# Transposes moved inside a projection half, a value product moved behind a branch unit, and one wait on Pool moved down

## The chip, the cores and the metric

The kernel runs on one core of a Trainium2 chip. The metric is the device time of one execution in microseconds (us): the median of three runs. Engines are named as in the profile: PE is TensorE (PEld its weight loads), ACT is ScalarE, DVE is VectorE, POOL is GpSimd, SP is the engine that issues most DMAs.

## The reference

Two layers of a decoder trunk on 256 tokens of width 1024 (float32), then a final norm. Each layer adds a mixer block and a mixture of experts:

```
h = rmsnorm(x);  proj = h @ w_in                      # 1024 x 7076
y_a = dsa_attention(...)        # 64 keys per query picked by an indexer, softmax
y_b = chunked_sgu(...)          # u * (tril(W_s) norm(v) + b)
y_c = stick_breaking_attention(...)
y_d = short_gated_conv(...)
merged = sum over n of sigmoid(gate_logits[n]) * (y_n @ w_branch[n])
x = x + merged @ w_out
x = x + hierarchical_moe(rmsnorm(x))   # top 1 of 4 groups, top 2 of its 8 experts
```

Stick-breaking attention forms, for head and query t, weights `A[t,s] = beta[t,s] * prod over s<j<t of (1 - beta[t,j])`, and multiplies them with the values. The gated branch is y_b.

## The kernel before

Tokens are held as two row tiles of 128 (`t` = 0, 1). The mixer's weights come as 36 units of 1 MB (`MIXER_UNITS`), each used in two halves `v` (unit u has halves 2u and 2u+1). A unit is either a slice of `w_in` (512 columns by four 128-row chunks), one branch's `w_branch`, or a quarter of `w_out`. Units come into a ring of nine slots. For each half, ACT rounds the weights to a high part (`hi_half`, line 1146), DVE forms the remainder (`lo_half`, line 1673, count `lo_done`), and PE multiplies in three passes (`three`, lines 492 to 494). Four halves of split weights are kept.

PE runs through a list written out by hand. `in_half(v, use)` waits until `lo_half(v)` is done, and then for each row tile issues six matmuls of 512 columns (two chunks, three passes); `use` picks PSUM banks 0 and 1, or 2 and 3. The first half of a block also waits that the block two uses back has been read out (`emptied`, count `block_out`). `wide_unit` multiplies a branch's output with its `w_branch`: twelve matmuls a half, into banks 0 and 1 and then 2 and 3; it has an `emptied` wait before each pair of banks.

Between these stand the small products of the attentions. Around the change the list is, in each layer:

```
                    in_half(32, 9)
                    pe.wait_ge(*L(zexp, 2))
                    p_transposes(zc, 1, 4)
                    pe.wait_ge(*L(yb_done, 1))
                    y_transposes(y_ab, 6)
                    in_half(33, 9)
```

Then come `pv(vc, 1, 7)` (16 small matmuls of weights by values into bank 7), `wide_unit(17)` (the branch product of y_b), `y_transposes(y_c, 5)`, `logits(qkT_a, 0, 6)`, units 18 and 19, units 20 and 21 (with `p_transposes(sc, 0, 6)` between them), and so on. `p_transposes(zc, 1, 4)` (line 602) turns the second row tile's stick-breaking weights, which ACT's exponential (`stick_exp(1)`, line 1188) has written; `y_transposes(y_ab, 6)` (line 487) turns y_b, which DVE's `sgu_gate` has written.

Every engine works through its own queue in its written order. DVE's queue around the change: `stick_sums(1)`, `y_evac_c(0)`, `sgu_gate`, `lo_half(33)`, `lo_half(34)`, `gate(0, 8)`, `yT_low(2, 1, 6)`, `lo_half(35)`, two rounds of `top_rounds` (the indexer's selection), `y_evac_c(1)` (line 1811: copies what `pv(vc, 1, 7)` made, count `y_out`), `gate(1, 9)` (line 1849), one more round, `lo(18)` (halves 36 and 37), `yT_low(3, 0, 5)` (line 1696, waits for ACT's `yT_high(2, 0, 5)`), two rounds, `lo(19)`, `sparse_logits(0, 6, sc)`, three rounds, `select_mask(1)`, `lo(20)`, `sparse_logits(1, 4, zc)`, `gate(2, 12)`, `lo(21)`, `lo(22)`.

ACT's queue: `stick_exp(1)`, `token_evac(8)` (line 1152: reads block 8 out of banks 0 and 1 through a sigmoid), `p_evac(2, 1, 4)`, `yT_high(1, 1, 6)` (line 1167), `hi_half(35)`, `token_evac(9)` (banks 2 and 3, after `gate(0, 8)`), `hi(18)`, `block_evac(10)` (after `gate(1, 9)`), `yT_high(2, 0, 5)`, `block_evac(11)`, `hi(19)`.

POOL adds the gated branches into `merged` (line 1560, count `gate_sum`); the fifth such sum is awaited by PE ahead of half 62, the first half of unit 31, which does not read `merged`; `m_transposes(0)` behind that half does.

Expert weights are loaded by SP's queue (lines 382 and 396) behind the mixer's units, each as its place comes free. They fill seven places for gate and up weights and nine for down weights before the first expert is computed.

Of the kernel before, what the change touches and what calls it, by code (L numbers as in the profile page):

```python
# [10 lines left out]
ACT = mybir.ActivationFunctionType  # L11
# [100 lines left out]
def build(nc, x_in, positions, norm1_g, w_in, sgu_ln_g, sgu_ln_b, w_spatial, b_spatial, conv_w, w_branch,  # L112
          w_out, norm2_g, w_rg, b_rg, w_re, b_re, w_eg, w_eu, w_ed, norm_f_g, out):
    ctx = ExitStack()
    with ctx:
# [306 lines left out]
        def preload_sqrt():  # L422

            nc.scalar.activation(spare, eps_t[:], ACT.Sqrt)

        def preload_gelu():

            nc.scalar.activation(spare, eps_t[:], ACT.Gelu_apprx_tanh)
# [40 lines left out]
        with nc.Block() as whole:  # L469

            @whole.tensor
            def _(pe):
# [7 lines left out]
                for l in range(DEPTH):  # L480
# [29 lines left out]
                    def in_half(v, use, layout="natural", between=None):  # L510

                        b0 = 2 * (use % 2)
                        h = MIXER_UNITS[v // 2][3]
                        n = unit_cols(v // 2)
                        pe.wait_ge(*L(lo_done, v + 1))
                        chunks = [(4 * h + 2 * (v % 2) + k, k) for k in range(2)]
                        begin, end = chunks[0][0] == 0, chunks[-1][0] == C - 1
                        if begin and use >= 2:
                            emptied(use - 2)
                        outs = []  # L520
                        if layout == "natural":
                            for t in range(TT):
                                outs.append((ps[:, b0 + t, 0:n], lambda c, k, t=t: h_tile(c, t),
                                             lambda c, k: w_tile(v, k, 0, n), True))
                        elif layout == "transposed":
                            for m in range(4):
                                outs.append((ps[:, b0 + m // 2, T * (m % 2):T * (m % 2) + T],
                                             lambda c, k, m=m: w_tile(v, k, P * m, P),
                                             lambda c, k: h_tile(c), m % 2 == 0))
                        else:  # L530
                            for t in range(TT):
                                outs.append((ps[:, b0, BW * t:BW * t + BW], lambda c, k, t=t: h_tile(c, t),
                                             lambda c, k: w_tile(v, k, 0, BW), t == 0))
                            for m in range(2):
                                outs.append((ps[:, b0 + 1, T * m:T * m + T],
                                             lambda c, k, m=m: w_tile(v, k, BW + P * m, P),
                                             lambda c, k: h_tile(c), m == 0))
                        if v < 4:
                            for c, k in chunks:
                                pe.wait_ge(*L(xT_lo, XT_GROUP_OF[c] + 1))  # L540
                                for dst, st, mv, opens in outs:
                                    ins = three(dst, st(c, k), mv(c, k), begin and k == 0 and opens,
                                                end and k == 1)
                                if k == 0 and between is not None:
                                    between()
                        else:
                            for dst, st, mv, opens in outs:
                                for c, k in chunks:
                                    ins = three(dst, st(c, k), mv(c, k), begin and k == 0 and opens,
                                                end and k == 1)  # L550
                        ins.then_inc(half_used, 1)

                    def in_unit(u, use, layout="natural"):
                        in_half(2 * u, use, layout)
                        in_half(2 * u + 1, use, layout)

                    def wide_unit(u, use, st, first_, last_):

                        for v in (2 * u, 2 * u + 1):
                            pe.wait_ge(*L(lo_done, v + 1))  # L560
                            final_half = v == 2 * NU - 1
                            order = [(hf, t) for hf in range(2) for t in range(TT)]
                            if final_half:
                                order.sort(key=lambda o: o[1])
                            for n, (hf, t) in enumerate(order):
                                if first_ and v % 2 == 0 and t == 0:
                                    emptied(use + hf - 2)
                                ins = three(ps[:, 2 * hf + t, :], st(v % 2, t), w_tile(v, 0, 512 * hf, 512),
                                            first_ and v % 2 == 0, last_ and v % 2 == 1)
                                if final_half and n == 1:  # L570
                                    ins.then_inc(mid_mm, 1)
                                elif first_ and last_ and v % 2 == 1 and n == 1:
                                    ins.then_inc(wide_mm, 1)
                            ins.then_inc(half_used, 1)
# [24 lines left out]
                    def p_transposes(src, t, b0):  # L599
                        for b in range(t + 1):  # L600
                            for h in range(NH):
                                ins = nc.tensor.transpose(ps[:, b0 + b, P * h:P * h + P],
                                                          src[:, h, P * b:P * b + P], ident[:])
                        ins.then_inc(pT_mm, 1)
# [10 lines left out]
                    def y_transposes(y, b0):  # L615
                        transposes([ps[:, b0, T * k + P * t:T * k + P * t + P]
                                    for k in range(2) for t in range(TT)],
                                   [y[:, t, P * k:P * k + P] for k in range(2) for t in range(TT)], yT_mm)

                    def y_tile(ring_at):  # L620
                        return lambda k, t: (yT_hi[:, ring_at, k, P * t:P * t + P],
                                             yT_lo[:, ring_at, k, P * t:P * t + P])
# [81 lines left out]
                    for g in range(NG):  # L704
                        ins = mm(ps[:, 6, P * g:P * g + P], wsT[:, g, :], vn[:, :, HD * g:HD * g + HD],
                                 start=(g == 0), stop=True, skip_group_check=True)
                    ins.then_inc(sgu_mm, 1)
                    in_half(32, 9)
                    pe.wait_ge(*L(zexp, 2))
                    p_transposes(zc, 1, 4)  # L710
                    pe.wait_ge(*L(yb_done, 1))
                    y_transposes(y_ab, 6)
                    in_half(33, 9)
                    pe.wait_ge(*L(pT_out, 2))
                    pe.wait_ge(*L(y_out, 1))
                    pv(vc, 1, 7)
                    pe.wait_ge(*L(yT_lo_out, 2))
                    wide_unit(17, 10, y_tile(1), True, True)
                    pe.wait_ge(*L(y_out, 2))
                    y_transposes(y_c, 5)  # L720
                    logits(qkT_a, 0, 6, la_mm)
                    in_unit(18, 12)
                    pe.wait_ge(*L(yT_lo_out, 3))
                    logits(qkT_a, 1, 4, la_mm)
                    in_unit(19, 12)
# [20 lines left out]
                    in_unit(28, 20)  # L746
                    in_unit(29, 20)
                    in_unit(30, 21)
                    pe.wait_ge(*L(gate_sum, 5))

                    def m_transposes(c0):
                        for b in range(2):
                            transposes([ps[:, 4 + c0 // 2 + b, T * k + P * t:T * k + P * t + P]
                                        for k in range(2) for t in range(TT)],
                                       [merged[:, t, P * (c0 + 2 * b + k):P * (c0 + 2 * b + k) + P]
                                        for k in range(2) for t in range(TT)], xT_mm)

                    in_half(62, 21)
                    m_transposes(0)
                    in_half(63, 21)  # L760
                    pe.wait_ge(*L(xT_lo, 7))
# [345 lines left out]
            def _(act):  # L1107
# [12 lines left out]
                for l in range(DEPTH):  # L1120
# [64 lines left out]
                    def stick_exp(t):  # L1185
                        w = P * (t + 1)
                        act.wait_ge(*L(zarg, t + 1))
                        A(zc[:, :, 0:w], zc[:, :, 0:w], ACT.Exp).then_inc(zexp, 1)
# [82 lines left out]
                    hi(16)  # L1271
                    hi_half(34, l)
                    stick_exp(1)
                    token_evac(8, sig, 0, ACT.Sigmoid)
                    p_evac(2, 1, 4)
                    yT_high(1, 1, 6)
                    hi_half(35, l)
                    act.wait_ge(*L(gate_prod, 1))
                    token_evac(9, sig, 2, ACT.Sigmoid)
# [330 lines left out]
            def _(dve):  # L1610
# [51 lines left out]
                for l in range(DEPTH):  # L1662
# [259 lines left out]
                    sgu_gate()  # L1922
                    lo_half(33)
                    lo_half(34)
                    gate(0, 8)
                    yT_low(2, 1, 6)
                    lo_half(35)
                    top_rounds(1, 2)
                    y_evac_c(1)
# [273 lines left out]
```

## Time and profile before

| | us |
|---|---|
| median of three runs (lowest, highest) | 889.68 (889.56, 890.39) |
| profiled execution, device time | 889.39 |
| its span, first to last instruction | 887.6 |
| PE busy in the span | 826.1 (93%) |
| DVE busy | 529.8 (60%) |
| ACT busy | 386.5 (44%) |
| POOL busy | 117.3 (13%) |

The mixer of the first layer takes the span from about 25 to 235 us, its experts up to about 443; the second layer follows with the same order. Times in the rows below are microseconds from the span's start. PE's 0.39 us for a matmul of 512 columns is its latency; one starts every 0.23 us.

### The profile page before, as it was taken

How to read it: one execution, taken by the hardware profiler on the slowest of the kernel's cores; microseconds unless marked ns; L12 is line 12 of the kernel's file. 1: busy time of each engine (PE TensorE's matmuls, PEld its weight loads, DVE VectorE, ACT ScalarE, POOL GpSimd, SP SyncE). 2: the span in 40 equal slices, each digit the busy share in tenths (PEclk: the TensorE clock that was granted, in tenths of full speed). 3: DMA queues.
4: the chain of work that ended last, by engine and by line, in shares of the span. 5: the costliest groups of instructions: out<-in, count | busy, mean ns of one | idle time of the engine just before them, and what ended most of it. 6: DMA issues, size and time to landing. Idle time of an engine off the chain costs nothing.

```text
span 887.6 us, 20367 instructions
## 1 busy us (share of the span) xinstructions
PE 826.1 (93%) x8763; PEld 662.0 (75%) x8763; DVE 529.8 (60%) x1067; ACT 386.5 (44%) x669; POOL 117.3 (13%) x169
## 2 busy tenths in 40 slices
PE   7999999999999998877999999999999999977984
PEld 7898878887897775655589977788789876654652
DVE  5768698667555555423376778976566455534434
ACT  5546868545422222111275568774454222211113
POOL 2840101212000000000066001022200000000000
PEclk9999999999999999978999999999999999999888
DMA  9966545498969999999998463555987999999994
GB/s 305 389 222 160 174 144 188 143 381 322 396 267 418 419 418 420 419 421 420 402 374 294 151 207 123 173 174 222 408 313 282 415 420 420 417 421 419 421 419 183
DMA packets 64125, 281.47 MB, mean 317 GB/s; under 512 B 5120, under 2 KB 7248, under 8 KB 39712
## 3 DMA queue, kind: packets, MB, share of 16 engines
q1 hardware_dynamic: 62752, 278.45, 80.1%
q0 software_dynamic: 800, 1.40, 1.2%
q8 instruction: 71, 1.16, 0.5%
q10 hardware_dynamic: 480, 0.28, 0.1%
q14 instruction: 22, 0.18, 0.1%
HBM read 279.06 MB, written 1.05 MB: 316 GB/s over the span
## 4 chain that ended last, share of the span: by engine, by line
PE 61%; DMA 20%; SPq 6%; issue 5%; ACT 3%; DVE 3%; POOL 1%; DVEq 0%; ACTq 0%; POOLq 0%
PE ps L492 12%; PE ps L494 11%; PE ps L493 11%; DMA ring<-in_w_exp_up 10%; PE ps L825 8%; DMA late<-in_w_exp_down 6%; PE ps L812 5%; PE ps L841 4%; SPq L382 4%; DMA late<-in_w_exp_up 3%; PE ps L925 2%; SPq L396 2%; DMA ring<-in_w_in 2%; POOL wide L1560 1%; PE ps L831 1%
## 5 line engine op out<-in xcount | busy, mean ns | idle before, releaser
L1673 DVE TENSOR_TENSOR split_lo<-ring,split_hi 128x1024 fp32r<-128x1024 f32 (+1 forms) x142 | 196.1, 1417 | 42.0 <-ACT split_hi L1146 40.8
L492 PE MATMUL ps<-split_hi,hT_hi 128*128 128x512 f32 (+2 forms) x416 | 161.4, 388 | 3.1 <-DVE hT_lo L1683 1.4
L1146 ACT ACTIVATE split_hi<-ring 128x1024 fp32r<-128x1024 f32 (+1 forms) x144 | 145.5, 1049 | 29.5 <-PE ps L494 27.3
L493 PE MATMUL ps<-split_lo,hT_hi 128*128 128x512 f32 (+2 forms) x416 | 157.6, 379 | 0.0
L494 PE MATMUL ps<-split_hi,hT_lo 128*128 128x512 f32 (+2 forms) x384 | 145.2, 378 | 0.0
L2085 DVE TENSOR_TENSOR wsT<-mb,ps 32x64 f32<-32x64 f32 x256 | 54.9, 215 | 141.2 <-ACT mb L1356 138.5
L1356 ACT ACTIVATE mb<-ps 128x64 f32<-128x64 f32 x64 | 14.3, 223 | 243.7 <-PE ps L825 243.7
L492 PEld LDWEIGHTS ps<-split_hi,hT_hi 128*128 128x128 f32 x416 | 78.2, 188 | 21.8 <-issue 3.7
L493 PEld LDWEIGHTS ps<-split_lo,hT_hi 128*128 128x128 f32 x416 | 78.3, 188 | 12.9
L494 PEld LDWEIGHTS ps<-split_hi,hT_lo 128*128 128x128 f32 x384 | 72.2, 188 | 13.3
L1577 POOL TENSOR_TENSOR idx<-idx,wt 128x128 f32<-128x128 f32 x32 | 12.1, 399 | 393.8 <-PE ps L847 309.8
L1383 ACT ACTIVATE first_down<-ps 32x256 f32<-32x256 f32 x112 | 41.8, 373 | 48.6 <-PE ps L841 48.0
L812 PEld LDWEIGHTS ps<-idx,wide 128*128 128x128 f32 x512 | 58.4, 192 | 5.8 <-issue 5.7
L812 PE MATMUL ps<-idx,wide 128*128 128x128 f32 x512 | 61.2, 278 | 0.0
L825 PE MATMUL ps<-ring,qkr 128*32 128x128 f32 x1536 | 51.7, 291 | 9.9 <-DMA ring<-in_w_exp_up 9.9
L825 PEld LDWEIGHTS ps<-ring,qkr 128*32 128x32 f32 x1536 | 44.9, 117 | 17.6 <-DMA ring<-in_w_exp_up 11.1
L2119 DVE COPY first_down<-ps 32x256 f32<-32x256 f32 x112 | 47.5, 424 | 14.6 <-PE ps L841 13.8
L825 PE MATMUL ps<-ring,yy 128*32 128x128 f32 x1344 | 45.1, 291 | 11.6 <-DMA ring<-in_w_exp_up 11.6
L1560 POOL TENSOR_TENSOR wide<-wide,qkr 128x1024 f32<-128x1024 f32 x10 | 33.1, 3310 | 165.2 <-DVE qkr L1849 165.2
L925 PE MATMUL ps<-first_down,wr 128*128 128x512 f32 x112 | 54.4, 618 | 0.0
L825 PEld LDWEIGHTS ps<-ring,yy 128*32 128x32 f32 x1344 | 39.2, 118 | 20.1 <-DMA ring<-in_w_exp_up 15.0
L2098 DVE TENSOR_TENSOR x<-x,ps 128x512 f32<-128x512 f32 x56 | 38.5, 688 | 15.7 <-PE ps L925 15.7
(278 smaller groups left out, 1317.9 us busy)
## 6 DMA issues: line engine op xcount, KB each, us to landing
ring<-in_w_in SPq DMA_DIRECT2D x52, 1024.0 KB, 10.0
ring<-in_w_exp_gate SPq DMA_DIRECT2D x45, 1024.0 KB, 24.5
ring<-in_w_exp_up SPq DMA_DIRECT2D x45, 1024.0 KB, 26.1
late<-in_w_exp_down SPq DMA_DIRECT2D x38, 1024.0 KB, 26.4
ring<-in_w_exp_down SPq DMA_DIRECT2D x15, 1024.0 KB, 26.7
new_pair<-in_w_exp_gate SPq DMA_DIRECT2D x10, 1024.0 KB, 18.6
new_pair<-in_w_exp_up SPq DMA_DIRECT2D x10, 1024.0 KB, 20.9
late<-in_w_exp_gate SPq DMA_DIRECT2D x9, 1024.0 KB, 24.6
```

The costliest lines, as they stand in the source:

```text
L492: mm(dst, st[0], mv[0], start=start, stop=False, skip_group_check=True)
L493: mm(dst, st[0], mv[1], start=False, stop=False, skip_group_check=True)
L494: return mm(dst, st[1], mv[0], start=False, stop=stop, skip_group_check=True)
L812: ins = mm(ps[:, b, P * c:P * c + P], wide[:, t, P * cc:P * cc + P], pick[:, t, :], start=(t == 0), stop=(t == TT - 1), skip_group_check=True)
L825: ins = mm(ps[32 * j:32 * j + 32, b, 0:P], hg[:, c, SLOTS * i:SLOTS * i + SLOTS], w[:, :, c, 64 * j:64 * j + 64], start=(c == 0), stop=(c ...
L925: mm(bank(banks[k]), scatT[:, t, :], y_slots[g % 2][:, 512 * hf:512 * hf + 512], start=True, stop=True).then_inc(scat_mm, 1)
L1146: A(half_view(split_hi[:, v % SPLITS, :], v), raw_half(v, l), ACT.Copy).then_inc(hi_done, 1)
L1383: ins = A(y_slots[g % 2][SLOTS * i:SLOTS * i + SLOTS, 256 * q:256 * q + 256], ps[32 * q:32 * q + 32, down_bank(e), 0:256], ACT.Copy)
L1560: nc.gpsimd.tensor_tensor(m, m, sig[:], ALU.add).then_inc(gate_sum, 1)
L1673: V.tensor_tensor(half_view(split_lo[:, v % SPLITS, :], v), raw_half(v, l), half_view(split_hi[:, v % SPLITS, :], v).bitcast(F32), ALU.sub ...
L2085: ins = V.tensor_tensor(hid[:, par, 64 * j:64 * j + 64], silu[32 * j:32 * j + 32, par, :], ps[32 * j:32 * j + 32, b, 64:128], ALU.mult)
L2119: ins = V.tensor_copy(y_slots[g % 2][SLOTS * i:SLOTS * i + SLOTS, 256 * q:256 * q + 256], ps[32 * q:32 * q + 32, down_bank(e), 0:256])
```

## The change

- PE: the transposes of y_b and of the second row tile's stick-breaking weights are put inside `in_half(33)`, between its two row tiles, with y_b's first; the function `in_half` gets a place for this.
- PE: `pv(vc, 1, 7)` is put behind `wide_unit(17)`. `y_transposes(y_c, 5)` and the first `logits(qkT_a, ...)` come behind the first half of unit 18 instead of ahead of it.
- PE: the wait for POOL's fifth sum is put behind `in_half(62)`.
- ACT: a small sigmoid on one column behind `stick_exp(1)`; `yT_high(1, 1, 6)` goes ahead of `token_evac(8)` and `p_evac(2, 1, 4)`.
- DVE: `yT_low(2, 1, 6)` goes ahead of `gate(0, 8)`. Nothing else of DVE's queue is changed.

```diff
+        def preload_sigmoid():
+
+            nc.scalar.activation(spare, eps_t[:], ACT.Sigmoid)
...
                         else:
-                            for dst, st, mv, opens in outs:
+                            for nth, (dst, st, mv, opens) in enumerate(outs):
+                                if nth == 1 and between is not None:
+                                    between()
                                 for c, k in chunks:
...
+                    def second_tile():
+                        pe.wait_ge(*L(yb_done, 1))
+                        y_transposes(y_ab, 6)
+                        pe.wait_ge(*L(zexp, 2))
+                        p_transposes(zc, 1, 4)
+
                     in_half(32, 9)
-                    pe.wait_ge(*L(zexp, 2))
-                    p_transposes(zc, 1, 4)
-                    pe.wait_ge(*L(yb_done, 1))
-                    y_transposes(y_ab, 6)
-                    in_half(33, 9)
+                    in_half(33, 9, "natural", second_tile)
+                    pe.wait_ge(*L(yT_lo_out, 2))
+                    wide_unit(17, 10, y_tile(1), True, True)
                     pe.wait_ge(*L(pT_out, 2))
                     pe.wait_ge(*L(y_out, 1))
                     pv(vc, 1, 7)
-                    pe.wait_ge(*L(yT_lo_out, 2))
-                    wide_unit(17, 10, y_tile(1), True, True)
+                    in_half(36, 12)
                     pe.wait_ge(*L(y_out, 2))
                     y_transposes(y_c, 5)
                     logits(qkT_a, 0, 6, la_mm)
-                    in_unit(18, 12)
+                    in_half(37, 12)
...
-                    pe.wait_ge(*L(gate_sum, 5))
...
                     in_half(62, 21)
+                    pe.wait_ge(*L(gate_sum, 5))
                     m_transposes(0)
...
                     stick_exp(1)
+                    preload_sigmoid()
+                    yT_high(1, 1, 6)
                     token_evac(8, sig, 0, ACT.Sigmoid)
                     p_evac(2, 1, 4)
-                    yT_high(1, 1, 6)
                     hi_half(35, l)
...
+                    yT_low(2, 1, 6)
                     gate(0, 8)
-                    yT_low(2, 1, 6)
```

## Rows read from the trace of the kernel before

**Rows 1.** Windows: stretch, its length, busy of PE, PEld, DVE, ACT, POOL, PEclk, DMA, GB/s.

```profile
128.00:160.00 32.00, 32.00 (x154) 25.78 (x153) 27.71 (x37) 25.20 (x40) 6.63 (x2) 1.00 0.48 164
```

**Rows 2.** Timeline of PE about unit 16: start, us, line, count, [idle before <- releaser].

```profile
114.10 1.09 PE L602 MATMUL ps<-ident,ring 128*128 128x128 f32 x8 [1.39 <-ACT ring L1188]
115.03 0.60 PE L487 MATMUL ps<-ident,yy 128*128 128x128 f32 x4
115.51 0.50 PE L492 MATMUL ps<-split_hi,hT_hi 128*128 128x512 f32 x1
...
118.37 1.89 PE L610 MATMUL ps<-first_down,ring 128*128 128x64 f32 x16
120.07 0.48 PE L492 MATMUL ps<-split_hi,yT_hi 128*128 128x512 f32 x1
...
548.24 1.09 PE L602 MATMUL ps<-ident,ring 128*128 128x128 f32 x8 [1.40 <-ACT ring L1188]
```

**Rows 3.** Timeline of DVE, unit 16's second half to unit 18's first.

```profile
114.25 2.35 DVE L1673 TENSOR_TENSOR split_lo<-ring,split_hi 128x1024 fp32r<-128x1024 f32 x2
...
122.11 0.42 DVE L1811 COPY yy<-ps 128x256 f32<-128x256 f32 x1
...
124.56 2.36 DVE L1673 TENSOR_TENSOR split_lo<-ring,split_hi 128x1024 fp32r<-128x1024 f32 x2
```

**Rows 4.** Timeline of ACT: the sigmoids of blocks 8 and 9.

```profile
115.36 1.27 ACT L1152 ACTIVATE qkr<-ps,scal 128x512 f32<-128x512 f32 x2
...
118.84 1.28 ACT L1152 ACTIVATE qkr<-ps,scal 128x512 f32<-128x512 f32 x2
```

**Rows 5.** Timeline of PE: y_c's transposes, then first matmuls of halves 36, 42 and 43.

```profile
125.65 0.60 PE L487 MATMUL ps<-ident,yy 128*128 128x128 f32 x4
...
126.82 0.50 PE L492 MATMUL ps<-split_hi,hT_hi 128*128 128x512 f32 x1
...
144.92 0.47 PE L492 MATMUL ps<-split_hi,hT_hi 128*128 128x512 f32 x1
...
147.86 0.50 PE L492 MATMUL ps<-split_hi,hT_hi 128*128 128x512 f32 x1
```

**Rows 6.** Timeline of DVE: `yT_low(3)`, `lo(20)`, `lo_half(43)`, then `y_evac_a(0)`.

```profile
126.91 0.69 DVE L1696 TENSOR_TENSOR yT_lo<-ps,yT_hi 128x512 fp32r<-128x512 f32 x1
...
137.02 2.36 DVE L1673 TENSOR_TENSOR split_lo<-ring,split_hi 128x1024 fp32r<-128x1024 f32 x2
...
144.37 3.44 DVE L1673 TENSOR_TENSOR split_lo<-ring,split_hi 128x1024 fp32r<-128x1024 f32 x1
...
151.75 0.49 DVE L1837 TENSOR_TENSOR yy<-ps,scal 128x128 f32<-128x128 f32 x2 [1.68 <-PE ps L610]
```

**Rows 7.** Timeline of POOL: the first and the fifth sum.

```profile
143.39 3.33 POOL L1560 TENSOR_TENSOR wide<-wide,qkr 128x1024 f32<-128x1024 f32 x1 [37.31 <-DVE qkr L1849]
...
201.94 3.29 POOL L1560 TENSOR_TENSOR wide<-wide,qkr 128x1024 f32<-128x1024 f32 x1 [13.55 <-DVE qkr L1849]
```

**Rows 8.** Timeline of PE ahead of half 62, and of DVE's `lo_half(63)`.

```profile
204.28 0.39 PE L494 MATMUL ps<-split_hi,hT_lo 128*128 128x512 f32 x1
205.28 0.50 PE L492 MATMUL ps<-split_hi,hT_hi 128*128 128x512 f32 x1 [0.60 <-POOL wide L1560]
...
202.91 3.40 DVE L1673 TENSOR_TENSOR split_lo<-ring,split_hi 128x1024 fp32r<-128x1024 f32 x1
```

**Rows 9.** Windows at the start of the first layer's experts (columns as in Rows 1).

```profile
248.00:250.00 2.00, 2.00 (x20) 2.00 (x19) 1.19 (x5) 0.00 (x0) 0.75 (x2) 1.00 0.00 0
```

**Rows 10.** Timeline of PE among the experts: 64 equal matmuls after waits of different length.

```profile
349.76 1.95 PE L825 MATMUL ps<-ring,yy 128*32 128x128 f32 x64 [1.30 <-DMA ring<-in_w_exp_up]
357.25 3.37 PE L825 MATMUL ps<-ring,yy 128*32 128x128 f32 x64 [3.94 <-DMA ring<-in_w_exp_up]
...
844.33 3.15 PE L825 MATMUL ps<-new_pair,yy 128*32 128x128 f32 x64 [2.07 <-DMA new_pair<-in_w_exp_up]
```

**Rows 11.** Windows after the wait that ended at 357.25 (columns as in Rows 1).

```profile
358.00:360.00 2.00, 2.00 (x44) 1.85 (x40) 0.00 (x0) 0.00 (x0) 0.00 (x0) 0.50 1.03 430
```

## Prediction

> **What bounds the kernel.** I read the windows by stage first, to see which engine is full where: in the mixer about the change PE is busy for the whole of a 32 us stretch at the full clock [rows 1]. The chain of waits there is PE after PE, so what is added to PE's queue or holds it lengthens the layer, unless the experts behind take it back. The waits of PE in the mixer name two that the change is aimed at: 1.39 us before the transposes of the stick-breaking weights, released by ACT's exponential [rows 2], and 0.60 us before half 62, released by POOL [rows 8]. Then I read the timelines of PE, DVE and ACT side by side about both, because PE's waits alone show only who came last, and not who would be next. Both layers do the same: the transposes start at 114.10 and at 548.24 with the same wait [rows 2], so what I work out for the first layer counts twice. POOL and SP issue nothing that is moved; no DMA is.
>
> **Step 1: the wait for the exponential goes, and DVE's remainder takes its place.** Half 33 needs `lo_half(33)`. DVE works two of these from 114.25 in 2.35 us, so the first is done about 115.45 [rows 3]. Half 33 started at 115.51 [rows 2], a few hundredths later. So the transposes stood in a gap in which PE could not have started half 33 anyway, and they are what filled it. After the change PE is free at 114.10 − 1.39 = 112.71 and still waits for 115.5: an idle of 2.8 us. Nothing on DVE ahead of that point depends on what is moved. Gain: 0.
>
> **Step 2: the transposes now cost their time.** They took from 114.10 to 115.51, 1.41 us. Inside half 33 they stand between matmuls for which all is ready. Both of their inputs are written by then. Half 33 ends at 118.37 + 1.41 = 119.8. Loss: 1.4.
>
> **Step 3: block 9's read-out is late for unit 17.** y_b's transposes now start after half of half 33 (its 12 matmuls took 118.37 − 115.51 = 2.86), at 116.94, and the last ends 0.60 later, at 117.5 [rows 2]. ACT waits for them with everything behind `yT_high(1)`: the sigmoid of block 8, `p_evac(2)`, `hi_half(35)`, the sigmoid of block 9. The same four items took 118.84 − 115.36 = 3.48 from the start of the first to the start of block 9's [rows 4], in another order. So block 9's sigmoid starts at about 117.6 + 3.5 = 121.1 and ends at 122.4. Unit 17 can start at 119.8 and wants banks 2 and 3 six matmuls later, at 121.2. Loss: 1.2. The small sigmoid itself costs nothing: it and its table load lie in ACT's idle between the exponential's end at 114.1 and 117.5; without that cover it would be the 1.3 us load, which is in ACT's queue before too. Unit 17 takes 125.65 − 120.07 = 5.58 [rows 2, 5] and ends at 119.8 + 1.2 + 5.6 = 126.6. `yT_low(2)`, earlier on DVE, is ready at about 118.9 and holds nothing.
>
> **Step 4: the value product now stands just ahead of half 36, with DVE's queue between them.** On DVE `y_evac_c(1)` is ahead of `gate(1, 9)`, one selection round and `lo_half(36)`. Before, the copy started at 122.11 and `lo(18)` at 124.56, 2.45 later, the first half done 1.2 after that [rows 3]; PE was at unit 17 meanwhile. Now the product starts at 126.6, PE is free of it 1.70 later at 128.3, and its result is there 1.89 after its start, at 128.5 [rows 2]. Half 36 can start at 128.5 + 2.45 + 1.2 = 132.2. PE idles 3.9 us. `block_evac(10)`, which half 36 also needs, waits for the same `gate(1, 9)`; it would be done at about 131.3, so it is the next in line and not the last. y_c's transposes and the first logits (126.82 − 125.65 = 1.17 [rows 5]) are only exchanged with half 36. PE is now 1.4 + 1.2 + 3.9 = 6.5 late.
>
> **Step 5: DVE is later than PE, and PE meets it again.** `yT_low(3)` started 126.91 − 125.65 = 1.26 after y_c's transposes [rows 5, 6]. These now come after half 36, at 132.2 + 2.8 = 135.0, so `yT_low(3)` starts at 136.3, 9.4 later than before. DVE idles from 133.4 till then, since its queue is in order. From `yT_low(3)` to `lo_half(43)` DVE had no gap before: it did `lo_half(43)` until 144.37 + 3.44 = 147.81, and PE started half 43 at 147.86 [rows 5, 6]. With no slack there, PE's lag of 6.5 must grow to DVE's 9.4: I expect 1.9 before half 40 (there the slack was 0.9: `lo_half(40)` done at 137.02 + 1.2 = 138.2, and the half started two halves of 2.7 and four transposes of 0.4 before 144.92, at 139.1), and 0.4 each before halves 42 and 43. After that DVE idled 1.68 before `y_evac_a(0)` [rows 6], so PE leads again and the lag stays at 9.4. Loss in steps 2 to 5 together: 9.4 a layer.
>
> `lo_half(43)` counts with 3.44, as in its row, and not with 1.22: it ran beside POOL's sum, which began at 143.39 for 3.33 us [rows 6, 7], and this sum moves with `gate(2, 12)`. The Trainium skill, SBUF — State Buffer, in its part on engine ports, calls the port pair of VectorE and GpSimd an exclusive lock, where the loser blocks fully. By that rule the remainder would run only when POOL is done, at 146.72, and end at 147.9, which the trace bears out at 147.81; had the two shared it instead, or not met, the sum would be up to 0.4 a layer less.
>
> **Step 6: the wait for POOL.** Unit 30 is issued to 204.28 + 0.23 = 204.51, half 62 started at 205.28. `lo_half(62)` was done when `lo_half(63)` began, at 202.9, so half 62 can follow at once. POOL's sum was done at 205.23 [rows 7], before the half's end at 207.3; `lo_half(63)` at 202.91 + 3.40 = 206.31 [rows 8], in time too. Nobody else's order changes. Gain: 0.8 a layer. If that cover were gone, the gain would be 0 and nothing lost.
>
> **Step 7: TensorE's clock.** The idles of 2.8 and 3.9 us are new to the mixer; the longest there was 1.39, with the clock at 2.4 GHz on both sides. Among the experts 64 matmuls took 1.95 after an idle of 1.30, but 3.15 after one of 2.07 and 3.37 after one of 3.94 [rows 10], at a granted clock of 0.50, the level of 1.2 GHz [rows 11]. All ten idles over 2 us there were followed by such a slow group. A fall costs 1.2 to 1.4 by these rows. Bounds for the two new idles: 0 (stay at full clock, as after 1.39) and 1.7 each; I take 1.3 each, since 3.9 is at the row of 3.94 and 2.8 lies between the rows of 2.07 and 3.94. What PE loses there, the transposes behind it, ACT and DVE lose too, so it adds to the 9.4. For the 1.9 before half 40 I take nothing.
>
> The Trainium skill, TensorE: Matmul & The Clock Gate, on HAM oscillation, says that a TensorE left waiting falls back to half rate and pays again for each such wait, a rule that speaks against this change; the same page warns that where the switch falls varies from run to run. By the rule the sum has the 2.6, without it not. The trace agrees in the 3.15 and 3.37 against 1.95.
>
> **Do the experts take the lag back?** Their stretch is limited by loads in part. But when the first is computed, the DMA share is 0.00 [rows 9]: all places are full, and the next load waits for the first expert. So the loads are late by what PE is late, and the lag stays whole.
>
> **The sum.** A layer: 1.4 + 1.2 + 3.9 + 2.9 = 9.4, less 0.8, plus 2.6, is 11.2. Two layers: 22.4. Against the profiled execution's 889.4 that gives 911.8; it lies 0.3 under the median of the runs, so I say 912.
>
> **Rivals.**
> - The clock stays up, or falls once a layer: 889.4 + 2 × 8.6 = 906.6, or 909.2. For it: before these idles PE was denser than among the experts. Against: ten of ten.
> - More queues meet: the first softmax or the sigmoids of blocks 12 and 13 become late too, or the clock falls a third time (1.9 before half 40). Another 2 to 3 a layer: 916 to 918. Against: `p_transposes(sc, 0, 6)` stands two units behind its logits.
> - The other side: the experts absorb it. Place: the first loads of the experts, issued behind the mixer. If DMA were behind when the experts start, a mixer later by 11 us would let the loads gain as much against PE. It decides once DMA has 11 us of loads pending at that start; then the time is 889.4 or under, 888. Against it: the share of 0.00.
> - The change does what it is aimed at: `lo_half(33)` is ready early, the 1.4 and the 0.8 go, and the product finds DVE ahead: 889.4 − 2 × 2.2 = 885. Against: 115.45 beside 115.51, and the order of DVE's queue.
>
> **How the numbers follow.** Forecast 50%, clock better 30%, more queues 14%, absorbed 3%, works as aimed 3%. The range reaches from 904 (no fall of the clock, 906.6, and step 3 at nothing, 2 × 1.2 less) to 917. Runs of this kernel can be told apart from about 0.2%, 1.8 us. Faster 0.04 (the last rival, and most of the absorbed case), same 0.02, slower 0.94.
>
> **What would show it.** After the change PE's waits should have: about 2.8 before half 33, released by DVE's split_lo; about 1.2 inside unit 17, released by ACT's sigmoid (qkr); about 3.9 before half 36, released by split_lo; about 2 before half 40, both layers; none on POOL's sum. DVE should idle about 4 before `y_evac_c(1)` and about 3 before `yT_low(3)`. The granted clock should show 0.50 behind half 33's and half 36's start. The forecast is wrong if half 36 starts within 1 us of the product's end, or if the experts' loads start earlier against the first expert than before.

## The result, and the profile after

The changed kernel takes 913.38 us (median of five runs, 912.68 to 915.11) against 889.66 for the kernel before, a ratio of 1.027 (95% interval 1.0256 to 1.0284): 24 us slower. Forecast were 912, slower, in a range of 904 to 917. The profiled execution took 913.89 with a span of 912.2, 24.6 more than before.

What PE waited for in the first layer's mixer, in the changed kernel (engine, line and tile, what released it: us in total, times, longest):

```profile
PE ps L496 <- DVE split_lo L1684: 8.8, 5, 3.8
PE ps L496 <- ACT qkr L1162: 1.2, 1, 1.2
PE ps L496 <- issue: 0.2, 1, 0.2
```

The wait for the exponential [rows 2] is gone, and so is the one for POOL [rows 8]. In their place stand four waits for DVE's remainders and one for ACT's read-out of block 9. (The fifth wait for a remainder in the count, of 0.17 us, is the one ahead of the kernel's very first unit, at 24.13, which was 0.48 in the kernel before.) The timeline of PE shows where (start, us, line, shape, count, [idle before <- releaser]); lines 496 to 498 are the 492 to 494 of before, 491 the 487, 608 the 602, 616 the 610:

```profile
115.12 0.80 PE L496 MATMUL ps<-split_hi,hT_hi 128*128 128x512 f32 x1 [2.81 <-DVE split_lo L1684]
117.85 0.81 PE L491 MATMUL ps<-ident,yy 128*128 128x128 f32 x4
118.49 1.04 PE L608 MATMUL ps<-ident,ring 128*128 128x128 f32 x8
119.29 0.47 PE L496 MATMUL ps<-split_hi,hT_hi 128*128 128x512 f32 x1
120.75 0.40 PE L496 MATMUL ps<-split_hi,yT_hi 128*128 128x512 f32 x1
123.52 0.50 PE L496 MATMUL ps<-split_hi,yT_hi 128*128 128x512 f32 x1 [1.21 <-ACT qkr L1162]
127.74 1.89 PE L616 MATMUL ps<-first_down,ring 128*128 128x64 f32 x16
133.46 0.79 PE L496 MATMUL ps<-split_hi,hT_hi 128*128 128x512 f32 x1 [3.83 <-DVE split_lo L1684]
138.74 0.61 PE L491 MATMUL ps<-ident,yy 128*128 128x128 f32 x4
151.39 0.50 PE L496 MATMUL ps<-split_hi,hT_hi 128*128 128x512 f32 x1 [1.72 <-DVE split_lo L1684]
160.94 0.50 PE L496 MATMUL ps<-split_hi,hT_hi 128*128 128x512 f32 x1 [0.29 <-DVE split_lo L1684]
```

Five of the forecast's waits are to be read off: before half 33 (2.81), in unit 17 (1.21), before half 36 (3.83), before half 40 (1.72) and before half 43 (0.29). The 0.4 forecast before half 42 shows only as a larger distance: the half starts 0.62 after the four transposes ahead of it (156.97 to 157.59) and not 0.35. The second layer has the same five waits: 2.81, 1.00, 3.83, 1.73 and 0.33. DVE's own timeline has the two idles that answer to [rows 3] and [rows 6]:

```profile
113.86 2.35 DVE L1684 TENSOR_TENSOR split_lo<-ring,split_hi 128x1024 fp32r<-128x1024 f32 x2
119.33 0.69 DVE L1707 TENSOR_TENSOR yT_lo<-ps,yT_hi 128x512 fp32r<-128x512 f32 x1 [3.12 <-ACT yT_hi L1177]
129.73 0.42 DVE L1822 COPY yy<-ps 128x256 f32<-128x256 f32 x1 [4.32 <-PE ps L616]
130.08 1.21 DVE L1860 TENSOR_TENSOR wide<-qkr,br 128x1024 f32<-128x1024 f32 x1
132.18 2.36 DVE L1684 TENSOR_TENSOR split_lo<-ring,split_hi 128x1024 fp32r<-128x1024 f32 x2
140.02 0.69 DVE L1707 TENSOR_TENSOR yT_lo<-ps,yT_hi 128x512 fp32r<-128x512 f32 x1 [5.47 <-ACT yT_hi L1177]
```

DVE does nothing for 4.32 us while PE works on unit 17, then copies the product, and only then makes the remainder that PE has been waiting for. Its second idle, before `yT_low(3)`, is 5.47 where about 3 was forecast: the forecast had half 36 at full clock, and it took 2.4 longer. The windows of the same stretch (busy of PE, PEld, DVE, ACT, POOL, then PEclk, DMA, GB/s) show the clock after the two long idles:

```profile
114.00:116.00 2.00, 0.88 (x2) 0.78 (x3) 2.00 (x2) 1.17 (x2) 0.00 (x0) 0.71 0.00 0
116.00:118.00 2.00, 2.00 (x6) 1.41 (x6) 0.21 (x1) 0.00 (x0) 0.00 (x0) 0.50 0.90 272
132.00:134.00 2.00, 0.54 (x1) 0.50 (x2) 1.97 (x3) 0.35 (x1) 0.00 (x0) 0.50 0.01 4
134.00:136.00 2.00, 2.00 (x6) 1.56 (x5) 0.54 (x1) 0.00 (x0) 0.00 (x0) 0.50 0.28 53
136.00:138.00 2.00, 2.00 (x6) 1.51 (x6) 0.00 (x0) 0.00 (x0) 0.00 (x0) 0.50 0.88 344
138.00:140.00 2.00, 2.00 (x16) 1.41 (x14) 0.00 (x0) 0.61 (x2) 0.00 (x0) 0.81 0.33 135
```

At 0.50 (1.2 GHz) a matmul of 512 columns starts every 0.43 us and not every 0.23. The whole of half 36, from 133.46 to 138.74, ran so.

At the start of the experts the DMA share is 0.00 as before [rows 9], so no more loads were under way than before when PE reached the first expert:

```profile
260.00:262.00 2.00, 2.00 (x20) 2.00 (x19) 0.92 (x3) 0.00 (x0) 0.76 (x2) 1.00 0.00 0
```

**The lag term by term**, first layer, each from the start of half 33 so that the 0.39 by which this execution began earlier drops out:

| term | forecast | measured | how measured |
|---|---|---|---|
| transposes and first clock fall, half 33 | 1.4 + 1.3 | 2.8 | 120.75 − 115.12 = 5.63, before 2.86 |
| unit 17's wait | 1.2 | 1.4 | 127.74 − 120.75 = 6.99, before 5.58 |
| product to half 36 | 3.9 | 4.0 | 133.46 − 127.74 = 5.72, before 1.70 |
| second clock fall, half 36 | 1.3 | 2.4 | 138.74 − 133.46 = 5.28, before 129.68 − 126.82 = 2.86 |
| DVE's zero slack to half 43 | 2.9 | 2.9 | rest of 160.94 − 115.12 = 45.82, before 32.35 |
| lag at half 43 | 12.0 | 13.5 | |

In the second layer half 43 starts 46.10 after half 33 (607.67 and 561.57), before 32.34: a lag of 13.8. The two lags less 2 × 0.8 for POOL's wait are 25.7. The span grew by 24.6. Of the 1.1 between them 0.4 is the earlier start of this execution. Another 0.7 to 0.8 lies between half 43 and the first layer's routing: there the group of 22 matmuls took 2.70 here and 4.02 in the profile before, where the clock was low, but 0.86 of that came back as a wait for DVE right behind it, so the group itself saves only 0.3 (its start to the next matmul: 3.55 and 3.86).

### The profile page after: what moved, and what is told of

It reads as the page before. It is cut to its first block, busy times and chain, and to the rows that moved or that the text cites. A ratio compares the mean times of both kernels' runs of the same rounds, so it can differ in the third digit from the quotient of the medians.

```text
span 912.2 us, 20367 instructions
## 1 busy us (share of the span) xinstructions
PE 833.7 (91%) x8763; PEld 664.8 (73%) x8763; DVE 529.6 (58%) x1067; ACT 386.8 (42%) x671; POOL 117.3 (13%) x169
## 4 chain that ended last, share of the span: by engine, by line
PE 58%; DMA 20%; DVE 9%; SPq 7%; ACT 4%; issue 2%; DVEq 0%; ACTq 0%
PE ps L496 12%; PE ps L498 11%; PE ps L497 11%; DMA ring<-in_w_exp_up 9%; PE ps L835 7%; DMA late<-in_w_exp_down 6%; SPq L382 5%; PE ps L822 4%; PE ps L851 3%; DMA late<-in_w_exp_up 3%; DVE split_lo L1684 3%; SPq L396 2%; PE ps L935 2%; DMA ring<-in_w_in 1%; PE ps L841 1%
## 5 line engine op out<-in xcount | busy, mean ns | idle before, releaser
L496 PE MATMUL ps<-split_hi,hT_hi 128*128 128x512 f32 (+2 forms) x416 | 164.6, 396 | 18.9 <-DVE split_lo L1684 17.5
L497 PE MATMUL ps<-split_lo,hT_hi 128*128 128x512 f32 (+2 forms) x416 | 160.3, 385 | 0.0
L498 PE MATMUL ps<-split_hi,hT_lo 128*128 128x512 f32 (+2 forms) x384 | 148.0, 386 | 0.0
L1394 ACT ACTIVATE first_down<-ps 32x256 f32<-32x256 f32 x112 | 41.9, 374 | 51.3 <-PE ps L851 50.6
```

The source lines that it names most:

```text
L496: mm(dst, st[0], mv[0], start=start, stop=False, skip_group_check=True)
L497: mm(dst, st[0], mv[1], start=False, stop=False, skip_group_check=True)
L498: return mm(dst, st[1], mv[0], start=False, stop=stop, skip_group_check=True)
L1394: ins = A(y_slots[g % 2][SLOTS * i:SLOTS * i + SLOTS, 256 * q:256 * q + 256], ps[32 * q:32 * q + 32, down_bank(e), 0:256], ACT.Copy)
```

## The experiments

All times are medians; ratios are to the kernel before on the same chip, with 95% intervals.

**a1_pool.** Only the POOL wait is moved.

```diff
                     in_unit(30, 21)
-                    pe.wait_ge(*L(gate_sum, 5))
...
                     in_half(62, 21)
+                    pe.wait_ge(*L(gate_sum, 5))
                     m_transposes(0)
```

Expected: 

> The kernel before with only the wait for POOL's fifth sum moved behind half 62. Theory (DVE's queue and idle-driven clock carry the loss): this part is a pure gain of 0.77 a layer, 889.66 - 1.5 = 888.1, no PE wait on POOL's sum left. Rival (the wait only hands over to the next one, lo_half(62) or the sigmoid of block 21): 889.6, with a new PE wait of 0.6 within 5 us.

Measured: 887.52, ratio 0.9976 (0.9965 to 0.9987), 2.1 us faster. The waits of PE in the mixer are these; no wait on POOL is among them, and none has come in its place:

```profile
PE ps L602 <- ACT ring L1188: 1.4, 1, 1.4
PE ps L492 <- issue: 0.2, 1, 0.2
```

The theory holds: by the interval the gain is 1.2 to 3.1 us, and the expected 1.5 lies inside. This part of the change alone is a gain.

**a2_tile.** Only the transposes inside half 33, with the orders of ACT and DVE that belong to it.

```diff
                     in_half(32, 9)
-                    pe.wait_ge(*L(zexp, 2))
-                    p_transposes(zc, 1, 4)
-                    pe.wait_ge(*L(yb_done, 1))
-                    y_transposes(y_ab, 6)
-                    in_half(33, 9)
+                    in_half(33, 9, "natural", second_tile)
...
                     stick_exp(1)
+                    preload_sigmoid()
+                    yT_high(1, 1, 6)
                     token_evac(8, sig, 0, ACT.Sigmoid)
                     p_evac(2, 1, 4)
-                    yT_high(1, 1, 6)
```

Expected: 

> The kernel before with only the two transposes inside half 33 and the orders of ACT and DVE that go with them; the value product stays ahead of unit 17. Theory: half 33 starts no earlier (115.5), PE idles 2.8 before it and its clock falls; the product then waits 0.5 for p_evac; the final lag is 2.0 to 2.2 a layer from the order and 1.3 from the clock, 896.5 (894.0 without the clock). Rival (the transposes are hidden there, and the whole loss is the value product's): 887 to 890.

Measured: 895.29, ratio 1.0064 (1.0049 to 1.0079), 5.7 us slower. The 5.7 are less than the expected 6.8 (7.6 in the profile). PE's waits in the first layer have 2.8 for DVE's remainder and no more than before elsewhere; the expected 0.5 before the product, for `p_evac`, is 0.33 in the second layer and not seen in the first:

```profile
PE ps L496 <- DVE split_lo L1683: 2.8, 1, 2.8
PE ps L496 <- POOL wide L1570: 0.6, 1, 0.6
```

Half 43 starts 3.4 us later after half 33 than before in the first layer and 3.6 in the second, where 3.3 to 3.5 was expected. The rival falls: the transposes are not hidden inside half 33. What was hidden is the place where they stood before.

**a3_pv.** Only the value product behind unit 17, with the exchange of y_c's transposes, the first logits and half 36.

```diff
-                    pe.wait_ge(*L(pT_out, 2))
-                    pe.wait_ge(*L(y_out, 1))
-                    pv(vc, 1, 7)
                     pe.wait_ge(*L(yT_lo_out, 2))
                     wide_unit(17, 10, y_tile(1), True, True)
+                    pe.wait_ge(*L(pT_out, 2))
+                    pe.wait_ge(*L(y_out, 1))
+                    pv(vc, 1, 7)
+                    in_half(36, 12)
...
-                    in_unit(18, 12)
+                    in_half(37, 12)
```

Expected: 

> The kernel before with only the value product behind unit 17 and y_c's transposes and the first logits behind half 36. Theory: PE idles 3.8 before half 36, released by DVE's remainder, the clock falls (2.5 a layer, as measured in the changed kernel), DVE's yT_low(3) is 7.2 late by order and 9.7 in all; 889.66 + 19.4 = 909. Rival (the loss is only what PE idles there, 3.8 a layer): 897.5.

Measured: 909.17, ratio 1.0219 (1.02 to 1.0238), 19.5 us slower, the number expected; the rival's 897.5 falls. On PE's timeline the idle and the slow half behind it (130.04 to 134.89, with y_c's transposes next) stand alone, without the transposes' part of the change:

```profile
124.31 1.89 PE L610 MATMUL ps<-first_down,ring 128*128 128x64 f32 x16
130.04 0.80 PE L492 MATMUL ps<-split_hi,hT_hi 128*128 128x512 f32 x1 [3.83 <-DVE split_lo L1674]
134.89 0.60 PE L487 MATMUL ps<-ident,yy 128*128 128x128 f32 x4
147.53 0.50 PE L492 MATMUL ps<-split_hi,hT_hi 128*128 128x512 f32 x1 [1.72 <-DVE split_lo L1674]
157.07 0.50 PE L492 MATMUL ps<-split_hi,hT_hi 128*128 128x512 f32 x1 [0.34 <-DVE split_lo L1674]
```

Half 36 took 4.85 here and not the 5.28 of the changed kernel, so the clock's fall cost 2.0 behind the same idle of 3.83. The three parts add up within their intervals: 5.7 + 19.5 − 2.1 = 23.1, where the whole change costs 24. Four fifths of the loss is the value product's new place.

**a4_dve.** The changed kernel, with DVE's copy of the product out of the way of the remainder.

```diff
-                    y_evac_c(1)
                     gate(1, 9)
                     top_rounds(1, 1)
                     lo(18)
+                    y_evac_c(1)
```

Expected: 

> The changed kernel with DVE's copy of the product (y_evac_c(1)) behind lo(18) instead of ahead of gate(1, 9). Theory: half 36 follows the product at once, no second fall of the clock; yT_low(3) is 5.5 late by order plus 1.3 for the first fall, less 0.8: 6.0 a layer, 901.7. Rival (PSUM banks: half 36 waits for the read-out of unit 17's banks by ACT, block_evac(10), whatever DVE's order): still 913.

Measured: 899.87, ratio 1.0116 (1.0099 to 1.0133): 13.5 of the 24 us come back by exchanging lines on DVE alone. Half 36 now follows the product at once, at full clock (2.86 us to the transposes):

```profile
127.17 1.89 PE L616 MATMUL ps<-first_down,ring 128*128 128x64 f32 x16
128.87 0.48 PE L496 MATMUL ps<-split_hi,hT_hi 128*128 128x512 f32 x1
131.73 0.60 PE L491 MATMUL ps<-ident,yy 128*128 128x128 f32 x4
144.37 0.50 PE L496 MATMUL ps<-split_hi,hT_hi 128*128 128x512 f32 x1 [1.70 <-DVE split_lo L1684]
```

The bank rival falls: the read-out of unit 17's banks by ACT holds nothing once `gate(1, 9)` is not behind the copy. The time is 1.8 better than expected, and the clock accounts for most of it. The idle before half 33 is 2.8 in both layers. In the first the clock fell only during half 33's first matmuls, and unit 17 waited 0.37 and not 1.2; in the second it did not fall at all. At half 43 the lags are 6.4 and 5.6 where 6.8 was expected. The window of the second layer, from half 33 to unit 17's wait (columns as in [rows 1]):

```profile
555.00:561.00 6.00, 5.71 (x30) 4.50 (x30) 3.19 (x4) 3.91 (x6) 0.00 (x0) 1.00 0.54 175
```

**b1_warm and d1_warm.** The changed kernel with matmuls whose results nobody reads in the two long idles, 20 and 30 in b1, 11 and 16 in d1:

```diff
+                    pe.wait_ge(*L(y_out, 1))
+                    keep_warm(11, 7)
                     in_half(33, 9, "natural", second_tile)
...
                     pv(vc, 1, 7)
+                    keep_warm(16, 6)
                     in_half(36, 12)
```

Expected of b1: 

> The changed kernel with matmuls of ones by the unit matrix (results unused) issued in PE's two long idles: 20 ahead of half 33, 30 ahead of half 36. They change no order on ACT or DVE. Theory (the idles also cost a fall of the clock, 1.3 before and 2.5 behind half 36 in a layer): the granted clock stays at 1.00 there, half 36 takes 2.8 instead of 5.3, and only the order's 9.4 less 0.8 a layer is left: 913.4 - 7 = 906.5. Rival (the slower matmuls are hidden behind DVE, which is the bound from yT_low(3) on): 913, clock 1.00 or not.

Measured: 917.43, ratio 1.032 (1.0304 to 1.0336), slower than the changed kernel. The clock stayed at 1.00, but I had sized the filling wrongly: one call is two matmul instructions on the array in float32, so the fillings took 4.5 and 6.7 us where the idles are 2.8 and 3.8, and they held halves 33 and 36 themselves:

```profile
113.02 4.73 PE L463 MATMUL ps<-ident,ones 128*128 128x128 f32 x40 [0.65 <-DVE yy L1825]
130.42 6.92 PE L463 MATMUL ps<-ident,ones 128*128 128x128 f32 x60
```

This run tells nothing on the clock's price; d1 has fitting counts.

Expected of d1: 

> As b1_warm, with 11 and 16 matmuls, since one of them takes PE 0.23 us and not 0.12. Theory: half 33 and half 36 start as in the changed kernel (115.5 and the end of DVE's remainder), the clock stays at 1.00, half 36 takes 2.8: 906.5. Rival (DVE hides the slow matmuls): 913.

Measured: 909.54, ratio 1.0227 (1.0213 to 1.0241). Half 36 starts when DVE allows and takes 136.38 − 133.50 = 2.88 us instead of 5.28. Half 33 has no wait on DVE in its row: it starts 3.1 after the half before it ended, and not 2.8, so the filling held it by 0.3 in each layer:

```profile
127.78 1.89 PE L616 MATMUL ps<-first_down,ring 128*128 128x64 f32 x16
129.51 3.79 PE L463 MATMUL ps<-ident,ones 128*128 128x128 f32 x32
133.50 0.50 PE L496 MATMUL ps<-split_hi,hT_hi 128*128 128x512 f32 x1 [0.20 <-DVE split_lo L1687]
136.38 0.60 PE L491 MATMUL ps<-ident,yy 128*128 128x128 f32 x4
158.58 0.50 PE L496 MATMUL ps<-split_hi,hT_hi 128*128 128x512 f32 x1 [0.34 <-DVE split_lo L1687]
```

From half 33 to half 43 (116.61 to 158.58) it takes 42.0 where the changed kernel took 45.8 with the falls; in the second layer 41.9 and 46.1. Less the 0.3 by which the filling held half 33, the two layers gain 3.5 and 3.9. With the clock at full, half 43 lies 9.9 later than in the kernel before, counted from the end of half 32 in each, in both layers; less the 0.3, that is 9.6 where the prediction had 9.4 for the order alone. So the clock's price is shown in the mixer. By the ratios only 3.8 of the expected 7 came out at the end (1.0270 to 1.0227), in the two profiles 4.6. Of the difference 1.2 stands at the very start of the kernel (the first wait on a weight unit ends at 25.32, in the changed kernel at 24.13). The kernels do not differ there, and in the ten profiles that show this wait it ends anywhere from 24.13 to 25.32, so this part need not be the filling's. Another 0.4 lies between the mixers and 1.2 behind the second one. What causes these, no run settles.

**b2_lo33.** The changed kernel with half 33's remainder made earlier on DVE.

```diff
+                    lo_half(33)
                     y_evac_c(0)
                     sgu_gate()
-                    lo_half(33)
```

Expected: 

> The changed kernel with DVE's lo_half(33) ahead of y_evac_c(0) and sgu_gate. Theory (step 1: half 33 starts when this remainder is done): half 33 starts 1.4 earlier, after an idle of 1.4 and not 2.8, the clock doesn't fall there, so 2.6 a layer come back: 908. Rival (half 33 is held by the exponential or y_b as before): no earlier start, 913.

Measured: 908.11, ratio 1.0209 (1.0196 to 1.0222): the number expected. Half 33 starts after an idle of 1.45, and its first six matmuls take 1.49 at full clock, in both layers:

```profile
113.66 0.50 PE L496 MATMUL ps<-split_hi,hT_hi 128*128 128x512 f32 x1 [1.45 <-DVE split_lo L1684]
115.15 0.60 PE L491 MATMUL ps<-ident,yy 128*128 128x128 f32 x4
```

So step 1 holds: DVE's remainder was the next thing late, behind the exponential that the profile named.

**b3_hi35.** The changed kernel with ACT's rounding of half 35 in an earlier idle.

```diff
                     hi_half(34, l)
+                    hi_half(35, l)
                     stick_exp(1)
...
                     p_evac(2, 1, 4)
-                    hi_half(35, l)
```

Expected: 

> The changed kernel with ACT's hi_half(35) ahead of stick_exp(1), in a stretch where ACT idles. Theory (step 3: unit 17's second pair of banks waits for block 9's sigmoid, which stands behind everything that follows y_b's transposes): the PE wait of 1.2 in unit 17 shrinks by 0.95 and passes on to the end: 911.5. Rival (later waits take it up, since half 36 waits for DVE anyway): 913.4.

Measured: 912.85, ratio 1.0252 (1.0236 to 1.0268), 1.6 us by the ratios, in the direction of the theory, but the intervals of the two kernels overlap (1.0256 is the changed kernel's lower end). By time alone it is inconclusive. The trace shows the wait in unit 17 at 0.76 in the first layer and 0.29 in the second, from 1.21 and 1.00, where it was to shrink by 0.95. In the first layer block 9's sigmoid now waits 0.38 for DVE's `gate(0, 8)`, which took over part of the wait. That supports that it hangs on ACT's queue; that it passes on to the end is not shown by this run.

**c1_best and d2_best.** From the kernel before, with a1's edit, to hide the exponential's wait in another way: `lo_half(33)` goes ahead of `stick_sums(1)`, so that half 33 fills the wait; the sigmoid of block 8, ready long before, goes into ACT's idle; `gate(2, 12)` goes behind `lo(21)`. d2 also splits the selection rounds about `lo_half(35)`.

```diff
                     in_half(32, 9)
+                    in_half(33, 9)
                     pe.wait_ge(*L(zexp, 2))
                     p_transposes(zc, 1, 4)
                     pe.wait_ge(*L(yb_done, 1))
                     y_transposes(y_ab, 6)
-                    in_half(33, 9)
...
-                    stick_exp(1)
                     token_evac(8, sig, 0, ACT.Sigmoid)
+                    stick_exp(1)
+                    preload_sigmoid()
                     p_evac(2, 1, 4)
                     yT_high(1, 1, 6)
-                    hi_half(35, l)
                     act.wait_ge(*L(gate_prod, 1))
                     token_evac(9, sig, 2, ACT.Sigmoid)
+                    hi_half(35, l)
...
                     lo_half(32)
+                    lo_half(33)
                     stick_sums(1)
                     y_evac_c(0)
                     sgu_gate()
-                    lo_half(33)
...
                     yT_low(2, 1, 6)
+                    top_rounds(1, 1)
                     lo_half(35)
-                    top_rounds(1, 2)
+                    top_rounds(1, 1)
...
-                    gate(2, 12)
                     lo(21)
+                    gate(2, 12)
```

(The two lines of `top_rounds` are d2's alone.) Expected of c1: 

> The kernel before with the POOL wait moved, DVE's lo_half(33) ahead of stick_sums(1), half 33 ahead of the transposes, ACT's sigmoid of block 8 in the idle ahead of the exponential and hi_half(35) last, and gate(2, 12) behind lo(21), so that lo_half(43) does not meet POOL's sum. Theory: the 1.39 wait goes, unit 17 starts 0.85 earlier and DVE no longer holds half 43: 0.9 + 0.8 a layer, 889.2 - 3.4 = 885.8. Rival (p_evac and yT_low are as late as before): 887.6, that is, only the POOL part's gain.

Measured: 887.66, ratio 0.9981 (0.9971 to 0.9990), no better than a1. The theory's 885.8 failed, and the rival's 887.6 came out. PE's waits say why: 0.9 before the product for `p_evac`, as the rival has it, and 0.8 before half 36 for DVE (the profiled execution took 890.68, 3 us above the median; both layers show the same waits).

```profile
PE ps L614 <- ACT ring L1175: 0.9, 1, 0.9
PE ps L496 <- DVE split_lo L1678: 0.8, 1, 0.8
```

Expected of d2: 

> c1_best with one of DVE's selection rounds ahead of lo_half(35), where DVE idled 1.4, and one behind. Theory (c1 lost its gain in a 0.8 wait of half 36 for lo_half(36)): that wait goes, 887.6 - 1.6 = 886.0. Rival (another wait takes its place, or the gain stays in the experts' loads): 887.6.

Measured: 886.20, ratio 0.9965 (0.9951 to 0.9978). The 0.8 is gone; the 0.9 for `p_evac` stays. It has the lowest median of all the kernels, 1.3 below a1 (1.0 by the ratios), but the two intervals overlap (0.9965 is a1's lower end); that it beats the kernel before is shown, that it beats a1 is not.

**d3_fixed.** The changed kernel with the other engines' queues fitted to it: a4's, b2's and b3's edits together, and

```diff
-                    yT_low(3, 0, 5)
                     top_rounds(1, 2)
+                    yT_low(3, 0, 5)
```

Expected: 

> The changed kernel with the queues of the other engines fitted to it: lo_half(33) ahead of y_evac_c(0), hi_half(35) ahead of stick_exp(1), y_evac_c(1) behind lo(18), the two rounds ahead of yT_low(3). Theory (the loss lies in the queues of DVE and ACT, not in PE's new order itself): a lag of 1.7 less 0.8 a layer is left and no fall of the clock: 891. Rival (PE's order itself costs, by the transposes between matmuls and the exchanged logits): 897 or more.

Measured: 893.90, ratio 1.0054 (1.0040 to 1.0067), between the two numbers. 19 of the 24 us come back without touching PE's order. PE's waits in the mixer:

```profile
PE ps L496 <- DVE split_lo L1684: 2.8, 3, 1.5
PE ps L496 <- ACT qkr L1162: 0.7, 1, 0.7
```

I had left out that `lo(19)` now waited 1.10 for ACT's rounding, which stands behind `yT_high(2)` and so behind half 36. DVE has no other idle from there to `lo(20)`, so the 1.02 before half 40 is that. At half 43, counted from the end of half 32, a layer is 3.1 later than before. Of this 2.1 are the waits of 0.75, 1.02 and 0.33; the idle before half 33 and the transposes together took 2.7 and before 2.8. So most of what is left of the loss is again queues and not the transposes' cost as such.

## Why the prediction was right

Its direction, its size and its steps held. Point by point:

- **Step 1** (the exponential's wait has DVE's remainder hidden behind it): right. The idle was forecast at 2.8 and is 2.81; b2 moved the remainder alone and got the 1.4 and the clock back.
- **Steps 2 and 3** (transposes 1.4, unit 17's wait 1.2): right. The transposes took 1.2 where the clock stayed at full (118.08 to 119.31 in d1), 0.2 less than the step read from the kernel before, and unit 17's wait is 1.21 in the trace. a2 has steps 1 and 2 alone, with the first fall of the clock, and costs 5.7.
- **Step 4** (the product just ahead of half 36): right, 3.83 for 3.9. a4 took the copy out of the way and half 36 followed at once.
- **Step 5** (PE meets DVE again at zero slack): right, 2.9 for 2.9, seen as waits of 1.72 and 0.29 before halves 40 and 43. The part on the port shared by DVE and POOL was not separated in the changed kernel; in c1 and d2, where `gate(2, 12)` comes later, the pair of `lo(21)` took 2.35 together and the slow remainder moved to the pair behind.
- **Step 6** (POOL's wait, 0.8 a layer): right in the trace; a1 measured 2.1 (1.2 to 3.1) for both layers where 1.6 was forecast.
- **Step 7** (clock): right that it fell at both idles of the changed kernel; the size of the second was wrong. The term was 1.3 and it measured 2.4 in both layers, above even the bound of 1.7. The step priced a fall by one group of 64 short matmuls [rows 10], and the price can run on behind the group. The profile before shows this too: after an idle of 2.68 the clock was at 0.50 from 388.5 to 394.2, so that the next group of 16 took 1.93, where it takes 1.07 at full clock:

```profile
388.49 3.64 PE L825 MATMUL ps<-ring,qkr 128*32 128x128 f32 x64 [2.68 <-DMA ring<-in_w_exp_up]
392.44 1.93 PE L841 MATMUL ps<-ring,mb 128*32 128x256 f32 x16
```

  The first fall cost 1.4 to 1.5 (half 33 with its transposes, against d1), near the forecast. But a fall behind 2.8 us is no certainty: a4's second layer had none.
- **The nearness of 912** is in part luck. At half 43 the lags are 3.2 above the forecast in the two layers together, 2.2 of it the second fall; 1.1 came back by the earlier start of the profiled execution and by the first layer's routing, neither of which was forecast.
- **The experts** take nothing back: share 0.00 at their start, as forecast. From behind the first layer's group of 22 matmuls to the second layer's half 33 it took 304.8 in the changed kernel and 304.4 before.

Of the rivals, "clock stays up" was excluded for the changed kernel by its windows, "the experts absorb" by the DMA share, "works as aimed" by a2 and a3, which each lose. "More queues meet" was partly true in size, through the clock and not through a new queue.

What stays open: why the filled idles of d1 gave 3.8 at the end and 7.4 in the two mixers, whether b3's gain is real, and what decides if the clock falls behind an idle of 2.8.

## What to carry to other kernels

A wait names the one that came last; before moving work out of its way, read on the other engines' timelines who would have come next, because work standing in a wait is free there and is paid for wherever it is put. When a product moves down one engine's list, find its consumer in the other engine's queue and count what is queued behind it: here a 0.4 us copy in front of a remainder cost more than all else. Edit the queues on both sides together, or not at all.

## What was not expected of the hardware

- After the same idle of 3.83 us before half 36 the half's first matmuls ran at 0.50 each time, but the clock did not come back after a fixed time. The 12 dense matmuls of 512 columns took 5.3 us in both layers of the changed kernel and of b2, 4.9 in both layers of a3, and 5.3 and 4.4 in the two of b3. After 2.81 before half 33 the clock fell in both layers of the changed kernel, of a2 and of b3, and in only one of the two layers of a4. After 1.45 (b2, d3) it did not fall.
- One float32 matmul of 128 columns by the unit matrix counts as two instructions (40 rows for 20 calls) and takes 0.23 to 0.24 us at full clock.
- POOL's sum of 128x1024 took 3.33 us when it met a DVE operation on its way in [rows 7], and 2.41 in d2, where DVE was idle when it began. There the next remainder on DVE was the slow one, so the two hinder each other in both directions:

```profile
144.88 1.22 DVE L1854 TENSOR_TENSOR qkr<-qkr,br 128x1024 f32<-128x1024 f32 x1
146.52 4.27 DVE L1678 TENSOR_TENSOR split_lo<-ring,split_hi 128x1024 fp32r<-128x1024 f32 x2 [0.43 <-ACT split_hi L1150]
...
146.17 2.41 POOL L1565 TENSOR_TENSOR wide<-wide,qkr 128x1024 f32<-128x1024 f32 x1 [39.83 <-DVE qkr L1854]
```
